# Dealing out a depthwise convolution's steps anew, unrolling four attention heads, and regrouping late conditioning loads

## The chip, the core and the metric

The kernel runs on one core of a Trainium2 chip. A core has TensorE (PE, matrix products into PSUM; PEld is its weight load), VectorE (DVE), ScalarE (ACT), GpSimd (POOL) and SyncE (SP), each with its own instruction queue, and 16 DMA engines that they share. The engines wait for each other through semaphores. The metric is the device time of one execution in microseconds, here the median of 3 runs; lower is better.

## The reference, cut to what matters

One decoder layer on 512 prompt tokens and 8 single-token samples, D_MODEL = 1024, all in float32:

```python
mod = c_act @ w_ada + b_ada                       # 9 x 1024 columns, conditioning of 3 norms and 3 gates
x = x + 0.5 * gt1 * swiglu(modulate(rms_norm(x), sh1, sc1), ...)
h = modulate(rms_norm(x), sh2, sc2)
ca, cb, q, k, v, r, a_lr, g_conv, g_gla = split(h @ w_in)
u = ca * sigmoid(cb)
d = causal_depthwise_conv(u, buf, conv_w) + conv_b           # 31 taps per channel
y_conv = silu(layer_norm(d)) @ w_conv_out
o, s_new = gla_chunked(q * HK ** -0.5, k, v, log_a, s0)      # 4 heads of linear attention
y_gla = (rms_norm(o) * silu(r)) @ w_gla_out
x = x + gt2 * ((sigmoid(g_conv) * y_conv + sigmoid(g_gla) * y_gla) @ w_out)
x = x + 0.5 * gt3 * swiglu(modulate(rms_norm(x), sh3, sc3), ...)
y = modulate(rms_norm(x), shf, scf)               # shf, scf = c_act @ w_ada_final + b_ada_final
```

## The kernel before, in words

Activations lie transposed in SBUF as 8 tiles (KT) of 128 channels by 520 columns (512 prompt tokens and 8 samples). The weights of every projection are worked through in *units*: one unit is 128 output channels, made of 48 matmuls of 260 columns (`unit`, L567 to L581; the matmuls show as L580). Each float32 operand is split into a high and a low part, and three products are formed. So a unit needs two weight tiles: `w_hi`, a cast on ACT (L1045), and `w_lo`, a subtraction on DVE (L1418) that waits for `w_hi`. Both are made in `step(n)`, which waits until unit n is done and then makes the weights of unit n+2 in the buffers that unit n has freed. PE therefore always has one unit in hand while the next but one is prepared. SP loads the raw weights, 1 MB for two units, and waits for `w_lo`.

The units of the mixing part come in this order: conv (16 units, which give u), qk (8), v (8), gates (24), then a layer norm over the convolution's output, yconv (8), ygla (8), out (8). What else happens is written by hand between the units of each engine:

- **The convolution.** It is done on DVE over four pairs of channel tiles. `conv_first(pair)` starts a pair with tap 0 (two instructions, L1706), and `conv_taps(pair, tap, count)` adds `count` taps, two instructions of 512 columns each (L1714, one per tile of the pair). Taps 1 to 30 of a pair follow each other. Pair 0 is done over the conv units, pair 1 over qk and v, pair 2 over v and gates, pair 3 over gates. Tables of counts, `TAPS_AT` (pair 3) and `TAPS2_AT` (pair 2), say how many taps follow each of the twelve gates units of a loop turn.
- **The decays** (`abs_z`, `log1p`, `decay`) run in the qk step: DVE makes |z|, ACT two passes of exp and ln for two heads at a time, DVE a scan over time.
- **The heads.** Six gates units (steps s = 0 to 5) go with each head. On every engine a hardware loop of two turns holds two heads each. Within a head DVE makes scaled copies of q and k (`diff`, `mix`), PE multiplies them (`gram`, L881), and DVE merges eight such results into the scores (`merge`, L1833). After unit s = 5 PE does the last two grams, then `prompt_o` (L941, L943), which waits for the eighth merge.
- **Conditioning.** The 44 slabs of 256 columns of `w_ada` and `w_ada_final` are multiplied with the conditioning vector. The first 32 go beside FFN 1. The last 12 (`LATE`) come in three stages of four slabs, at the norm before the mixing part, at the layer norm of the convolution, and at the norm before FFN 2. Of each stage `late_slabs` does the products on PE (L617), a copy brings the rows to SBUF, and `late_transposes` (L639) turns them into columns that DVE adds to `mod`. POOL loads the slabs into buffers that share memory with others: `raw_h`, the second half of stage 1, lies where `h_lo` is, which the gates units read until their end. So POOL waits for `s_done >= at["yconv"]` before that load.

After the last head the norm runs so: DVE adds up the eight tiles of d, PE sums over channels (L657), DVE subtracts the mean from each tile (L1941), ACT squares (L1346), PE sums the squares (L657), and ACT and DVE make the scale. On PE `late_slabs(1)` stands between the two sums.

Of the kernel before, what the change touches and what calls it, by code (L numbers as in the profile page):

```python
# [18 lines left out]
F32 = mybir.dt.float32  # L19
# [7 lines left out]
P = 128  # L27
# [26 lines left out]
TAPS_AT = [1, 2, 1, 1, 2, 0, 1, 2, 1, 2, 2, 0]  # L54
TAPS2_AT = [0, 0, 1, 1, 1, 2, 0, 0, 1, 1, 1, 0]
# [66 lines left out]
LATE_BANK = [0, 2, 0]  # L122
# [17 lines left out]
def decoder_step(nc, a, o):  # L140
# [3 lines left out]
    with ExitStack() as ctx:  # L144
# [22 lines left out]
        raw_h, h_lo = overlay(("raw_h", [P, 2, KT, 256], F32), ("h_lo", [P, KT, N], F32R))  # L167
# [40 lines left out]
        rows, o_hi, u = overlay(("rows", [P, 2 * D + 4 * P], F32), ("o_hi", [P, KT, N], F32R),  # L208
# [4 lines left out]
        rows_a, rows_l = lb[:, 0:2, 0:256], lb[:, 2:4, 0:NP]  # L213
# [41 lines left out]
        LATE = [((raw_a, "a1"), (raw_q, "q")), ((raw_v, "v2"), (raw_h, "h")), ((raw_a, "a3"), (raw_v, "v3"))]  # L255
# [30 lines left out]
        s_late = {k: sem("late_slabs_loaded_" + k) for k in ("a1", "q", "v2", "h", "a3", "v3")}  # L286
# [136 lines left out]
        def _(pool):  # L423
# [63 lines left out]
            def late_load(stage, two):  # L487

                dst, name = LATE[stage][two]
                for j in range(2):  # L490
                    m = LATE0 + 4 * stage + 2 * two + j
# [4 lines left out]
            late_load(0, 1)  # L496
            pool.wait_ge(s_ad, LATE0)
            late_load(0, 0)
# [25 lines left out]
            for h in range(HEADS):  # L524
                pool.wait_ge(s_S, 4 * h + 4)
                pool.dma_start(o["gla_p"][0, 0, h], SB[:, 3, :]).then_inc(s_So, 16)
                if h + 1 == HEADS:
                    pool.wait_ge(s_gk, HEADS)
                    late_load(1, 0)
# [22 lines left out]
            late_load(2, 0)  # L552
            late_load(2, 1)
# [5 lines left out]
        def _(pe):  # L559
# [61 lines left out]
            def late_slabs(stage):  # L621

                for two in range(2):
                    src, name = LATE[stage][two]
                    pe.wait_ge(s_late[name], 32)
                    for j in range(2):
                        last = slab_rows(src[:, j], 2 + two, 256 * j)
                    last.then_inc(s_lb, 1)

            def late_transposes(stage):  # L630

                pe.wait_ge(s_mod, LATE0 + 4 * stage)
                pe.wait_ge(s_lr, 2 * stage + 2)
                if stage == 1:
                    pe.wait_ge(s_or, 1)
                else:
                    pe.wait_ge(s_rstd, stage + 2)
# [105 lines left out]
            def ffn(which):  # L743
# [12 lines left out]
                for g in range(3):  # L756
                    n0 = at[f"up{which}_{g}"]
                    for i, k in bodies(pe, GROUPS[g] // 2, g == 0):
                        if g == 0 and i is None:
                            unit_pair(Lin(n0), h_hi, h_lo, s_h, (which - 1) * 3 * KT, rest if which == 1 else None)  # L760
                            if which == 2:
                                late_transposes(2)
# [1309 lines left out]
```

## Time and profile before

| | |
|---|---|
| median of 3 runs | 1534.94 us (1529.86, 1534.94, 1537.53) |
| the profiled execution | 1534.01 us |
| its span | 1531.3 us, 30166 instructions |
| mean granted TensorE clock | 0.976 |
| busy: PE / DVE / ACT / POOL | 94% / 53% / 32% / 5% |

The span is what the trace covers; the 2.7 us between it and the execution's own time lie outside. Busy time is what an engine's instructions took. The clock is a share of full speed, 1.0 for 2.4 GHz and 0.5 for 1.2 GHz. L numbers are lines of the kernel before.

### The profile page before, as it was taken

The page shows a single profiled execution, that of the slowest core. Times are in us where ns is not written, and L with a number is a line of the kernel's source. Part 1 is how long each engine was busy: PE and PEld are TensorE (multiplying, and loading weights), DVE is VectorE, ACT ScalarE, POOL GpSimd, SP SyncE. Part 2 cuts the span into 40 slices and gives each one's busy share as a digit, 9 for nine tenths or more (in the row PEclk, how much of TensorE's full clock was granted, in tenths as well). Part 3 has the DMA queues.
Part 4 walks back from the last instruction along what each step waited for, and adds up shares of the span by engine and source line. Part 5 has one row for each costly group of instructions (what it writes and reads, how often), then busy time and mean ns, then how long its engine had stood idle before and what let it go on. Part 6 is the DMA issues. An engine that isn't in the chain of part 4 may idle for free.

```text
span 1531.3 us, 30166 instructions
## 1 busy us (share of the span) xinstructions
PE 1445.2 (94%) x11974; PEld 1395.4 (91%) x11974; DVE 817.1 (53%) x1362; ACT 483.0 (32%) x651; POOL 75.8 (5%) x112
## 2 busy tenths in 40 slices
PE   6999999999998999999988995999989999999995
PEld 5899999999997999988988894999989999999994
DVE  5423332333365785999696795765552332333345
ACT  5322122212245225233323234522342212221233
POOL 6100000010000000000000001000000000000000
PEclk9999999999999999999999998999999999999997
DMA  9754545474232222222332445334313223223211
GB/s 308 228 185 137 192 138 185 138 260 127 68 100 87 83 92 78 83 83 94 132 116 80 138 149 168 136 115 154 125 52 107 85 83 103 89 83 99 87 62 56
DMA packets 133332, 187.10 MB, mean 122 GB/s; under 512 B 4571, under 2 KB 113519, under 8 KB 133214
## 3 DMA queue, kind: packets, MB, share of 16 engines
q1 hardware_dynamic: 112396, 112.54, 23.1%
q0 software_dynamic: 16800, 64.85, 12.7%
q10 hardware_dynamic: 4050, 8.53, 1.5%
q8 instruction: 59, 0.97, 0.3%
q14 instruction: 27, 0.22, 0.0%
HBM read 172.44 MB, written 14.41 MB: 122 GB/s over the span
## 4 chain that ended last, share of the span: by engine, by line
PE 53%; DVE 9%; issue 4%; ACT 2%; DMA 1%; DVEq 1%; POOL 0%; ACTq 0%
PE pu L580 45%; PE pu L596 3%; DVE d L1714 1%; DVE w_lo L1418 1%; DMA raw_h<-in_w_ada_final 1%; ACT w_hi L1045 1%; PE pg L657 1%; DVE work L1833 1%; DVE work L1842 1%; PE pg L941 1%; PE pg L881 1%; DVE work L1826 0%; PE pg L995 0%; DVE sg L1547 0%; DVE work L1814 0%
## 5 line engine op out<-in xcount | busy, mean ns | idle before, releaser
L1418 DVE TENSOR_TENSOR w_lo<-raw,w_hi 128x1024 fp32r<-128x1024 f32 x216 | 264.2, 1224 | 575.5 <-ACT w_hi L1045 575.4
L580 PE MATMUL pu<-h_hi,w_hi 128*128 128x260 f32 x2432 | 497.7, 286 | 12.3 <-issue 6.5
L580 PE MATMUL pu<-h_hi,w_lo 128*128 128x260 f32 x2432 | 492.4, 284 | 0.0
L580 PE MATMUL pu<-h_lo,w_hi 128*128 128x260 f32 x2432 | 491.3, 284 | 0.0
L1045 ACT CAST w_hi<-raw 128x1024 fp32r<-128x1024 f32 x216 | 225.8, 1046 | 664.3 <-PE pu L580 648.1
L580 PEld LDWEIGHTS pu<-h_hi,w_hi 128*128 128x128 f32 x2432 | 377.6, 190 | 17.7 <-issue 10.5
L580 PEld LDWEIGHTS pu<-h_hi,w_lo 128*128 128x128 f32 x2432 | 377.3, 190 | 0.0
L580 PEld LDWEIGHTS pu<-h_lo,w_hi 128*128 128x128 f32 x2432 | 376.7, 189 | 0.0
L1714 DVE SCALAR_TENSOR_TENSOR d<-u,cw,d 128x512 f32<-128x512 f32 x240 | 162.7, 743 | 0.0
L580 PE MATMUL pu<-f_hi,w_hi 128*128 128x260 f32 x704 | 142.6, 284 | 2.0 <-DVE f_lo L1669 2.0
L580 PE MATMUL pu<-f_hi,w_lo 128*128 128x260 f32 x704 | 141.8, 283 | 0.0
L580 PE MATMUL pu<-f_lo,w_hi 128*128 128x260 f32 x704 | 141.3, 282 | 0.0
L580 PEld LDWEIGHTS pu<-f_hi,w_hi 128*128 128x128 f32 x704 | 108.3, 188 | 4.1 <-DVE f_lo L1669 2.5
L580 PEld LDWEIGHTS pu<-f_hi,w_lo 128*128 128x128 f32 x704 | 108.4, 188 | 0.0
L580 PEld LDWEIGHTS pu<-f_lo,w_hi 128*128 128x128 f32 x704 | 108.3, 188 | 0.0
L1176 ACT CAST f_hi<-sg 128x520 f32 (+1 forms) x44 | 27.6, 627 | 87.8 <-DVE sg L1666 87.8
L1669 DVE TENSOR_TENSOR f_lo<-sg,f_hi 128x520 f32 (+1 forms) x44 | 30.8, 701 | 40.4 <-ACT f_hi L1176 40.4
L596 PE MATMUL pu<-h_hi,w_hi 128*128 128x260 f32 x128 | 29.0, 312 | 11.7 <-DVE h_lo L1565 6.6
L1286 ACT ACTIVATE work<-work 128x512 f32<-128x512 f32 x28 | 17.7, 631 | 68.2 <-DVE work L1814 68.1
L881 PEld LDWEIGHTS pg<-work 128*128 128x128 f32 x224 | 27.1, 191 | 8.5 <-DVE work L1833 4.8
L596 PEld LDWEIGHTS pu<-h_hi,w_hi 128*128 128x128 f32 x128 | 22.2, 212 | 13.3 <-issue 13.0
L881 PE MATMUL pg<-work 128*128 128x128 f32 x224 | 30.6, 282 | 3.2 <-DVE work L1833 3.2
(283 smaller groups left out, 1287.7 us busy)
## 6 DMA issues: line engine op xcount, KB each, us to landing
raw_a<-in_w_ada POOLq DMA_DIRECT2D x30, 1024.0 KB, 7.8
raw<-in_w_in SPq DMA_DIRECT2D x28, 1024.0 KB, 5.2
raw<-in_ffn_up SPq DMA_DIRECT2D x22, 1024.0 KB, 5.4
raw<-in_ffn_gate SPq DMA_DIRECT2D x21, 1024.0 KB, 5.4
raw<-in_ffn_down SPq DMA_DIRECT2D x16, 1024.0 KB, 4.9
gates_d<-sg ACTq DMA_DIRECT2D x24, 260.0 KB, 2.1
raw<-in_ffn_down SPq DMA_DIRECT2D x8, 768.0 KB, 4.2
work<-gates_d POOLq DMA_DIRECT2D x2, 2080.0 KB, 11.4
```

Of the source, the lines that this page charges most:

```text
L580: last = mm(pu[p][:, e, 0:HALF], w[p][:, k, :], m[:, k, e * HALF:(e + 1) * HALF], start=(k == 0 and j == 0), stop=(k == k_tiles - 1 and j ...
L596: last = mm(pu[p][:, e, 0:HALF], w[p][:, k, :], m[:, k, e * HALF:(e + 1) * HALF], start=(k == 0 and j == 0), stop=(k == KT - 1 and j == 2))
L657: last = mm(ps[:, e, 0:HALF], ones[:], src[:, e * HALF:(e + 1) * HALF], start=start, stop=stop)
L881: last = mm(pg[:, l % 2, c * CH:(c + 1) * CH], m, m if rhs is None else rhs[:, c * CH:(c + 1) * CH], start=True, stop=True)
L941: last = mm(pg[:, 2 + t, cs], VH[:, c, ts], SC[:, cs], start=True, stop=(c == 0))
L1045: nc.scalar.copy(w_hi[p][:], raw[:, slot, :, p * P:(p + 1) * P]).then_inc(s_hi, 1)
L1176: nc.scalar.copy(tile(f_hi, Lin(2 * k0 + c - 2, 2, i).value()), sg[:, c - 2, :]).then_inc(s_ahi, 1)
L1286: af(E_[:, l % 2, :], E_[:, l % 2, :], ACT.Exp, scale=1 / 16).then_inc(s_ge, 1)
L1418: V.tensor_tensor(w_lo[p][:], raw[:, slot, :, p * P:(p + 1) * P], w_hi[p][:].bitcast(F32), ALU.subtract).then_inc(s_lo, 1)
L1669: V.tensor_tensor(tile(f_lo, t.value()), s, tile(f_hi, t.value()).bitcast(F32), ALU.subtract).then_inc(s_a, 1)
L1714: conv.mark(V.scalar_tensor_tensor(d[:, t, 0:NP], flat(u[:, t:t + 1, bass.ds(tap + s, NP)]), cw[:, bass.ds((tap + s) * KT + t, 1)], d[:, t ...
L1833: V.copy_predicated(SC.rearrange("p (c t) -> p c t", c=NC), masks[:, l:l + 1, :].bitcast(U16).to_broadcast([P, NC, CH]), pg[:, l % 2, :].r ...
```

## The change

Four things are done together.

1. **Taps.** The 120 taps stay, in the same order for each pair, but stand elsewhere on DVE: 18 instead of 14 in the qk step, 28 instead of 30 in the v step, 44 instead of 46 over the heads. Pair 1 starts with three taps ahead of the first qk unit and three more stand in qk's step 2. Over the heads one table now gives, for each of the six steps, 1, 1, 2, 2, 0, 7 taps in heads 0 to 2 and 1, 1, 2, 1, 0, 0 in head 3 (before: 1, 2, 2, 2, 3, 2 in heads 0 and 2, and 1, 2, 2, 3, 3, 0 in heads 1 and 3).
2. **Heads.** PE and DVE have their four heads written out instead of a loop of two turns with two heads each. ACT keeps its loop. The five additions of d at the end of a turn are now issued once, not twice.
3. **ACT's order.** In the qk step the second `log1p` comes after the next unit's cast and copy, not before. In the v step the copy out of PSUM of each fourth unit comes before the cast of the next weights.
4. **Late slabs.** Six slabs go over the first of the three norms, two over the layer norm, four over the last. `raw_h` is gone. The new buffer `raw_u` lies where `u` will be; POOL issues its load right after that of `raw_q`.

```diff
-TAPS_AT = [1, 2, 1, 1, 2, 0, 1, 2, 1, 2, 2, 0]
-TAPS2_AT = [0, 0, 1, 1, 1, 2, 0, 0, 1, 1, 1, 0]
+TAPS_AT = [1, 1, 2, 2, 0, 7] * 3 + [1, 1, 2, 1, 0, 0]
+TAPS_V = [(2, 2), (1, 2), (2, 2), (1, 2)]
-        LATE = [((raw_a, "a1"), (raw_q, "q")), ((raw_v, "v2"), (raw_h, "h")), ((raw_a, "a3"), (raw_v, "v3"))]
+        LATE = [(raw_a, "a1"), (raw_q, "q"), (raw_u, "u"), (raw_v, "v2"), (raw_a, "a3"), (raw_v, "v3")]
 # POOL
-            late_load(0, 1)
+            late_load(1)
+            pool.wait_ge(s_tp, 4 + KT)
+            late_load(2)
             pool.wait_ge(s_ad, LATE0)
-            late_load(0, 0)
+            late_load(0)
...
-                if h + 1 == HEADS:
-                    pool.wait_ge(s_done, at["yconv"])
-                    late_load(1, 1)
 # PE, first conv units
                     unit_pair(Lin(at["conv"]), h_hi, h_lo, s_h, KT)
-                    late_transposes(0)
-                    pe.wait_ge(s_mod, LATE0 + 4)
+                    pe.wait_ge(s_lr, 1)
+                    late_slabs(2)
+                    pe.wait_ge(s_rstd, 2)
+                    late_transposes(0, 1)
...
             a_rows()
+            late_transposes(2)
 # PE, heads
-            with pe.Fori(0, 2) as i:
-                for hh in range(2):
-                    h = Lin(hh, 2, i)
+            for hh in range(HEADS):
+                h = Lin(hh)
...
             pe.wait_ge(s_oe, 2 * HEADS)
-            late_slabs(1)
+            late_slabs(3)
 # ACT, qk and v steps
-                        if c >= 2:
-                            log1p((2 * c - 4, 2 * c - 3))
+                        if c == 2:
+                            log1p((0, 1))
+                    elif c == 0:
+                        log1p((2, 3))
...
-                    step(Lin(at["v"] + c, 4, i))
+                    n = Lin(at["v"] + c, 4, i)
+                    act.wait_ge(s_done, n.value(1, 1))
+                    if c < 3:
+                        step(n)
                     nc.scalar.copy(halves(sg[:, c, :]), psum(c % 2)).then_inc(s_evac[c % 2], 1)
+                    if c == 3:
+                        step(n)
 # DVE, qk step
             conv_first(1)
+            conv_taps(1, 1, 3)
...
                 if c == 1:
-                    conv_taps(1, 1, 2)
+                    conv_taps(1, 4, 2)
                 if c == 2:
                     abs_z(0)
                     abs_z(1)
+                    conv_taps(1, 6, 3)
...
-                conv_taps(1, 3 + 3 * c, 3)
-                if c == 0:
-                    decay(2)
-                    decay(3)
+                if c in (1, 2):
+                    decay(c + 1)
+                conv_taps(1, (9, 12, 13, 15)[c], (3, 1, 2, 4)[c])
 # DVE, heads
+            def gate_taps(done, count):
+
+                for k in range(done, done + count):
+                    if k < 14:
+                        conv_taps(2, 17 + k, 1)
+                    else:
+                        conv_taps(3, k - 13, 1)
...
-                        conv_taps(2, i * 8 + (15 + sum(TAPS2_AT[:c])), TAPS2_AT[c])
-                        conv_taps(3, i * 15 + (1 + done), more - done)
+                    gate_taps(sum(TAPS_AT[:6 * hh + s]), TAPS_AT[6 * hh + s])
 # DVE, layer norm
-            for two in range(2):
-                dve.wait_ge(s_lb, two + 3)
-                V.tensor_copy(rows_l[:, two], pg[:, 2 + two, :]).then_inc(s_lr, 1)
+            dve.wait_ge(s_lb, 4)
+            V.tensor_copy(rows_l[:, LATE_SLOT[3]], pg[:, LATE_ROWS[3], :]).then_inc(s_lr, 1)
```

How the instructions stand, at three places. DVE before, in head 0, from the last tap of step 4 over step 5 (`w_lo`, two merges) to its first tap:

```order
L102 REGISTER_ALU
L1714 ISA
L1714 SCALAR_TENSOR_TENSOR d<-u,cw,d 128x512
L1417 REGISTER_ALU
L1418 TENSOR_TENSOR w_lo<-raw,w_hi 128x1024
L1914 REGISTER_ALU
L1833 COPY_PREDICATED work<-masks,pg 128x512
L1831 REGISTER_ALU
L1833 COPY_PREDICATED work<-masks,pg 128x512
L102 REGISTER_ALU
L1714 ISA x2
L1714 SCALAR_TENSOR_TENSOR d<-u,cw,d 128x512
```

DVE now, in head 1, from the last merges of step 4 to the first unit of head 2 (taps are L1727, merges L1852, `w_lo` L1433):

```order
L1935 TENSOR_SCALAR work<-qk 128x512
L1852 COPY_PREDICATED work<-masks,pg 128x512
L1433 TENSOR_TENSOR w_lo<-raw,w_hi 128x1024
L1852 COPY_PREDICATED work<-masks,pg 128x512 x2
L1727 SCALAR_TENSOR_TENSOR d<-u,cw,d 128x512 x14
L1433 TENSOR_TENSOR w_lo<-raw,w_hi 128x1024
L1888 TENSOR_TENSOR work<-lb 128x512
```

The taps between merge 5 and `w_lo` have gone; fourteen tap instructions stand behind the eighth merge. The register instructions that worked out addresses from the loop's counter have gone too.

PE before, from the end of the loop over the heads to the layer norm's sums:

```order
L943 MATMUL pg<-work 128x128
L946 REGISTER_ALU
L946 COMPARE_AND_BRANCH
L657 MATMUL pg<-sg,ones 128x260 x2
L617 MATMUL pg<-raw_v,c_f 32x256 x16
L617 MATMUL pg<-raw_h,c_f 32x256 x16
L657 MATMUL pg<-sg,ones 128x260 x16
L995 MATMUL pg<-work,ones 128x260 x4
```

PE now:

```order
L946 MATMUL pg<-work 128x128
L948 MATMUL pg<-work 128x128
L655 MATMUL pg<-sg,ones 128x260 x2
L618 MATMUL pg<-raw_v,c_f 32x256 x16
L655 MATMUL pg<-sg,ones 128x260 x16
L999 MATMUL pg<-work,ones 128x260 x4
```

The products with `raw_h` have gone from here, and so has the branch. The products with `raw_u` now stand behind the first pair of conv units.

ACT before, in the qk step, from the copy of unit 3 (L1242) to that of unit 4 (`w_hi` is L1045, `log1p` L1232 and L1236):

```order
L1242 ACTIVATE qk<-pu 128x520
L1232 ACT_TABLE_LOAD
L1232 ACTIVATE sg<-sg 128x520 x2
L1236 ACT_TABLE_LOAD
L1236 ACTIVATE sg<-sg,ones 128x520 x2
L114 UNCONDITIONAL_BRANCH
L1045 CAST w_hi<-raw 128x1024
L1242 ACTIVATE qk<-pu 128x520
```

ACT now:

```order
L1250 ACTIVATE qk<-pu 128x520
L114 UNCONDITIONAL_BRANCH
L1051 CAST w_hi<-raw 128x1024
L1250 ACTIVATE qk<-pu 128x520
L1240 ACT_TABLE_LOAD
L1240 ACTIVATE sg<-sg 128x520 x2
```

The cast `w_hi` for the second next unit stands ahead of the exp and ln passes now.

## Rows read from the trace of the kernel before

**Rows 1.** Page, part 1: busy us (share of the span) xinstructions.

```profile
PE 1445.2 (94%) x11974; PEld 1395.4 (91%) x11974; DVE 817.1 (53%) x1362; ACT 483.0 (32%) x651; POOL 75.8 (5%) x112
```

**Rows 2.** Windows: length, busy (x instructions) per engine, PEclk, DMA share, GB/s.

```profile
612.00:620.00 8.00, 6.19 (x39) 6.19 (x39) 7.43 (x13) 2.34 (x4) 0.00 (x0) 0.79 0.00 0
683.12:803.21 120.09, 112.56 (x867) 106.88 (x865) 101.71 (x184) 37.61 (x58) 4.74 (x6) 0.96 0.36 116
736.06:744.33 8.27, 5.86 (x29) 5.87 (x29) 4.75 (x7) 0.17 (x1) 0.92 (x1) 0.59 0.72 244
794.83:815.60 20.77, 13.34 (x79) 13.15 (x79) 6.46 (x9) 1.18 (x2) 1.78 (x2) 0.75 0.51 155
862.78:868.54 5.76, 3.38 (x31) 3.39 (x31) 4.72 (x7) 0.17 (x1) 0.90 (x1) 1.00 0.62 176
918.87:955.52 36.65, 21.02 (x137) 15.61 (x137) 19.63 (x30) 14.54 (x21) 4.07 (x5) 0.86 0.55 175
```

**Rows 3.** Timeline, PE, qk step: start, us, instruction, [idle before].

```profile
613.81 0.51 PE L580 MATMUL pu<-h_hi,w_hi 128*128 128x260 f32 x2 [2.05 <-DVE w_lo L1418]
622.92 0.51 PE L580 MATMUL pu<-h_hi,w_hi 128*128 128x260 f32 x2 [1.57 <-DVE w_lo L1418]
```

**Rows 4.** Timeline, DVE and ACT, the same step.

```profile
607.46 0.67 DVE L1762 SCALAR_TENSOR_TENSOR sg<-lb 128x520 f32<-128x520 f32 x1
612.53 1.23 DVE L1418 TENSOR_TENSOR w_lo<-raw,w_hi 128x1024 fp32r<-128x1024 f32 x1 [4.40 <-ACT w_hi L1045]
...
611.37 1.03 ACT L1045 CAST w_hi<-raw 128x1024 fp32r<-128x1024 f32 x1
```

**Rows 5.** Timeline, PE and ACT, v step.

```profile
654.76 0.63 PE L862 MATMUL pg<-ident,sg 128*128 128x128 f32 x4 [1.67 <-issue]
...
681.16 0.59 ACT L1261 COPY sg<-pu 128x520 f32<-128x520 f32 x1
```

**Rows 6.** Timeline, PE, heads 0 and 3.

```profile
712.38 1.16 PE L881 MATMUL pg<-work 128*128 128x128 f32 x8 [1.60 <-DVE work L1833]
...
922.17 1.22 PE L941 MATMUL pg<-work 128*128 128x128 f32 x4 [3.30 <-DVE work L1833]
```

**Rows 7.** Timeline, DVE, head 0, steps 4 and 5.

```profile
731.64 4.05 DVE L1714 SCALAR_TENSOR_TENSOR d<-u,cw,d 128x512 f32<-128x512 f32 x6
735.61 1.23 DVE L1418 TENSOR_TENSOR w_lo<-raw,w_hi 128x1024 fp32r<-128x1024 f32 x1
737.62 0.72 DVE L1833 COPY_PREDICATED work<-masks,pg 128x512 f32<-128x512 uint16 x1 [0.15 <-DVE work L1833]
751.44 1.22 DVE L1418 TENSOR_TENSOR w_lo<-raw,w_hi 128x1024 fp32r<-128x1024 f32 x1 [10.48 <-ACT w_hi L1045]
```

**Rows 8.** Chain that ended last: a whole unit, and the loop's jump back.

```profile
744.55 5.78 PE pu L580 x48
803.21 4.08 issue
807.28 8.31 PE pu L580 x48
```

**Rows 9.** The same chain, between the heads and the convolution's output matmul.

```profile
921.34 15.81 DMA raw_h<-in_w_ada_final
937.20 3.64 PE pg L617 x32
940.84 7.86 PE pg L657 x32
955.52 13.24 PE pu L596 x96
```

**Rows 10.** Timeline, DVE and ACT, the same place.

```profile
929.28 4.97 DVE L1941 TENSOR_TENSOR d<-d,sg 128x520 f32<-128x520 f32 x8
...
943.48 0.64 ACT L1346 ACTIVATE sg<-d 128x520 f32<-128x520 f32 x1 [0.24 <-PE pg L657]
```

**Rows 11.** DMA queue q8 (instructions), 683.1 to 803.2: packets, MB, share.

```profile
q8 instruction: 7, 0.11, 0.4%
```

More of the change, by code:

```diff
@@ L619, in slab_rows, with late_slabs, late_transposes @@
                 return last
-            def late_slabs(stage):
-                for two in range(2):
[L624 to L637, printed above, removed]
-                for j in range(8):
-                    last = mm(pg[:, LATE_BANK[stage], 10 * j:10 * j + 10], rows_l[:, j // 4, j % 4 * P:(j % 4 + 1) * P],
-                              sel[:], start=True, stop=True)
+            def late_slabs(g):
+                src, name = LATE[g]
+                pe.wait_ge(s_late[name], 32)
+                for j in range(2):
+                    last = slab_rows(src[:, j], LATE_ROWS[g], 256 * j)
+                last.then_inc(s_lb, 1)
+            def late_transposes(*groups):
+                pe.wait_ge(s_mod, LATE0 + 2 * groups[0])
+                pe.wait_ge(s_lr, groups[-1] + 1)
+                for g in groups:
+                    for j in range(4):
+                        c = 10 * (j + 4 * (g - groups[0]))
+                        last = mm(pg[:, LATE_BANK[g], c:c + 10], rows_l[:, LATE_SLOT[g], j * P:(j + 1) * P],
+                                  sel[:], start=True, stop=True)
                 last.then_inc(s_lt, 1)
@@ L778, in _ @@
             late_slabs(0)
+            late_slabs(1)
             def state_transposes(t0):
                 pe.wait_ge(s_ld["st"], 32)
-                pe.wait_ge(s_rstd, 2)
+                pe.wait_ge(s_mod, LATE0 + 4)
+                pe.wait_ge(s_lr, 3)
                 for t in range(t0, t0 + 4):
@@ L819, in _ @@
             a_rows()
+            late_transposes(2)
             def u_tails():
+                pe.wait_ge(s_mod, LATE0 + 6)
                 for p in range(2):
@@ L1721, in conv_units @@
                     step(n)
+                    if i is None and c == 1:
+                        late_out(0, 1)
+                        dve.wait_ge(s_lb, 3)
+                        chain.link(V.memset(u[:, :, 0:TAPS - 1], 0.0))
                     if c >= 2:
@@ L1739, in _ @@
             conv.end(3)
+            late_out(2)
             def sample_conv():
@@ L1789, in _ @@
                 step(Lin(at["qk"] + 4 + c))
-                conv_taps(1, 3 + 3 * c, 3)
-                if c == 0:
-                    decay(2)
-                    decay(3)
+                if c in (1, 2):
+                    decay(c + 1)
+                conv_taps(1, (9, 12, 13, 15)[c], (3, 1, 2, 4)[c])
             conv_first(2)
             with dve.Fori(0, 2) as i:
-                conv.loop(i, 30)
+                conv.loop(i, 28)
                 for c in range(4):
                     step(Lin(at["v"] + c, 4, i))
-                    conv_taps(1, i * 8 + (15 + 2 * c), 2)
-                    conv_taps(2, i * 7 + (1 + 2 * c), 2 if c < 3 else 1)
+                    for pair, at_0, per, j in ((1, 19, 6, 0), (2, 1, 8, 1)):
+                        conv_taps(pair, i * per + (at_0 + sum(t[j] for t in TAPS_V[:c])), TAPS_V[c][j])
             conv.end(2)
```

267 lines of the change are left out of this document (133 added, 134 removed).

## The prediction

> **What bounds the kernel now.** I read the page's busy times first. PE is busy 94% of the span and everything else far less [rows 1], so the kernel is as long as PE's work plus its pauses and its slow stretches. Next the chain that ended last: it runs through PE's units almost everywhere and leaves PE only in the mixing part, so I cut that part into stretches and asked of each how long PE stood and at which clock [rows 2]. A whole unit takes 5.78 us at full clock [rows 8]. Then the timelines say who ended each pause. The reader is to see five kinds of pause in these rows: two in the qk step that end with `w_lo` [rows 3, 4], one after each fourth v unit [rows 5], one in the middle of a head and one ahead of `prompt_o` that both end with a merge on DVE [rows 6], one where the loop over the heads jumps back [rows 8], and a long one at the layer norm that ends with the load of `raw_h` [rows 9]. After several of them the granted clock is at its lower level, 1.2 GHz: 0.79 on the mean over 612 to 620, 0.59 after the pause of head 0 [rows 2].
>
> **The qk step.** DVE has its last |z| ready at 607.46 + 0.67, then stands 4.40 us because ACT does both passes of `log1p` before it casts `w_hi` at 611.37 [rows 4]. Unit 5 ended at 613.81 - 2.05 = 611.8 and unit 4 one unit earlier [rows 3, 8], at 606, so with the cast first it is ready by 607.2 and `w_lo` follows at 608.1, well ahead of 611.8, when PE wants it. The 2.05 us go. The second pause, 1.57 us, came because three taps and two decays stood between two `w_lo`; now the decays stand one unit apart. Each of the next slots holds at most one `w_lo` (1.2) and three taps (six instructions, 4.05), or one `w_lo`, a decay (its instructions took about 2) and two taps (2.7), against 5.8 us of PE. The clock over the 8 us was 0.79: 0.21 of 8 us, 1.7 us, come back with the first pause. The six taps added earlier lie in idle time of DVE before units 0 and 3. Sum 2.05 + 1.57 + 1.7 = 5.3 us; bounds 3.6 (the clock stays as it was) and 5.4.
>
> **The v step.** PE stands 1.67 us for the copy that follows the cast [rows 5]. The copy takes 0.59 us, the cast 1.03 [rows 4, 5]. With the copy first the pause is 0.65; twice 1.0 is 2.0 us. The cast comes 0.6 us later, where the unit that wants it is 7 us away. The two taps fewer change nothing, since DVE is not waited for. Bounds 1.5 and 3.0.
>
> **Middle of heads 0 and 2.** PE waits 1.60 us for merge 0 in each [rows 6]. DVE works without a gap up to it, and one tap of two instructions less stands ahead of it: 4.05 / 6 = 0.675 us an instruction [rows 7], 1.35 us. 2 x 1.35 = 2.7 us; bounds 0 and 3.2.
>
> **Ends of heads 0, 1 and 2.** The three stretches run from the last small matmul before `prompt_o` [rows 2]. The first and third are 8.27 and 5.76 us and end with `prompt_o`; the second is 20.77 us and takes in the jump and the next unit. At full clock `prompt_o` keeps PE busy 3.38 us (third stretch, clock 1.00). The pause ahead of it is there because six tap instructions, 4.05 us, end at 735.6 and only then come `w_lo` and two merges [rows 7]. Without them `w_lo` is done before the last gram is, which ends about when the stretch begins less 1.1 us; two merges take 0.15 + 2 x 0.72 = 1.6, and leave a pause of 0.7 with their hand-over. So the first and third stretch become 0.7 + 3.4 = 4.1, and the second, whose 4.08 us of jump have gone and whose unit took 8.31 instead of 5.78 us [rows 8], becomes 4.1 + 5.8 = 9.9. Gain 4.2 + 1.7 + 10.9 = 16.8 us. The lower bound is 10 us: the three pauses shrink, the jump goes, and the clock falls as before. What is late next are the 14 tap instructions behind the eighth merge: 14 x 0.675 = 9.45 us, from 0.7 to 10.2 us after the stretch's begin. The `w_lo` behind them can start only when the next unit has ended and its `w_hi` is cast: 4.1 + 5.8 + 1.05 = 10.9. They fit with 0.7 us to spare, in a place where DVE stood for 10.48 us [rows 7]. The tap's mean over the page's list would be 0.743 us by the single instruction; pipelined in runs it is 0.675, and this is a run.
>
> **The layer norm.** From the end of the small matmuls of head 3 to the first matmul of yconv it is 36.65 us [rows 2]. Two things go. The pause of 3.30 us ahead of `prompt_o` [rows 6] shrinks to 0.7, and the additions of d follow the same merges, so all moves up by 2.6. And the load of `raw_h`, which lands at 937.15 [rows 9], is gone with its products. The squares' sums ended at 940.84 + 7.86 = 948.70. What is late next is the chain of the squares: the first centred tile is there at 929.28 + 4.97 / 8 = 929.9, its square 0.64 later, and then one sum each 0.64 + 0.24 = 0.88 us [rows 10]: 930.6 + 8 x 0.88 = 937.6. The remaining products with `raw_v` are over by 930.4, as now. So 948.7 - 937.6 = 11.1, with the 2.6 together 13.7 us. `raw_v` is issued when head 3's states are made, 24 us ahead of this place, and the reload of the gates (2 MB, 11.4 us in the page's list) is wanted after the pair of yconv units. Bounds: 8 us, if PE does the eight sums and the slabs at the lower clock after its short pauses, and 15.
>
> **The slabs themselves.** The layer norm's transposes shrink from 8 to 4, 0.8 us less. At the first norm two slabs and four transposes are added, 1.9 + 0.8 us, on PE. In turn PE no longer waits there for DVE to write `mod` (`s_mod` LATE0 + 4), which with the hand-over costs about the same. I take 0 for it, between a gain of 2 and a loss of 3. The load into `raw_u` is issued some hundred microseconds ahead of its use.
>
> **The sum.** 5.3 + 2.0 + 2.7 + 16.8 + 13.7 + 0.8 = 41.3 us. The profiled execution took 1534.01 us, 0.9 below the median shown; less 41.3 that is 1492.7. Forecast 1492.7 us. All low bounds together give 3.6 + 1.5 + 0 + 10 + 8 + 0.8 - 3 = 20.9, 1513; all high ones 5.4 + 3 + 3.2 + 18 + 15 + 0.8 + 2 = 47, 1487.
>
> **Rivals.** *First: DVE takes the place of the pauses in the heads.* In two heads it is busy 101.71 of 120.09 us now, and 184 instructions stand there [rows 2]. If the heads shorten to about 110 us and 26 taps instead of 23 stand in them, DVE is busy some 102 of 110 us. For it speaks that little is left for hand-overs, and that the seven taps fit with only 0.7 us. Against it: in steps 0 to 4, where PE waits for DVE's merges, DVE has 6 taps instead of 10. If the burst comes 2.5 us late at three ends, and the clock falls each time for another 1.7 us, 12.6 us are lost again: 1505.
>
> *Second: the layer norm keeps its length.* Another transfer or the low clock takes over from `raw_h`. For it: PE still has pauses of about 2 and 5 us there, and its clock over the whole stretch is 0.86 [rows 2]. Against it, nothing else waited for lands after 937. With 8 instead of 13.7, and the same caution at the heads' ends (10 instead of 16.8), the time is 1505 as well.
>
> *Third, on the other side: straight code stalls as the jump did.* PE's jump back costs 4.08 us of issue with nothing waited for, and the next unit 2.5 us of clock [rows 8], 6.6 together. The unrolled heads 2 and 3 are code that no one has fetched. During heads 0 and 1, q8 brought 7 packets of instructions [rows 11]. If each such packet stalled PE as the jump did, 7 x 6.6 = 46 us would be lost and 41.3 won: 1539. It decides from six such stalls on. Against it: heads 0 and 1 are run for the first time in that very stretch, with the 7 packets, and no pause of theirs over half a microsecond is "issue"; the price seems that of a jump to a place that isn't at hand, not of going on.
>
> The Trainium skill, "Advanced Engine Details and Errata", section ISA Cache, gives TensorE 128 KB in lines of 16 KB, 256 instructions each. By that figure the 867 matmuls and 865 weight loads of two heads are about 7 lines, as many as the q8 packets, which agrees with the trace. The same section says "Only 2 cache lines!". By that rule the code of heads 0 and 1 is never at hand when the loop returns, which fits the stall at the jump, and unrolled code would stall only if fetching ahead fails; the trace shows that it does not in heads 0 and 1.
>
> *Fourth: the change gives nothing*, because the pauses were ended by something else that stands as before. Nothing in the rows supports it; 1530.
>
> **Chances.** Forecast 0.74, first rival 0.10, second 0.08, third 0.05, fourth 0.03. A range of 1484 to 1511 holds the first three cases and leaves out less than 2 in 10. I count about 0.5% (7.7 us) as what can't be told from no change. Faster 0.92, the same 0.04, slower 0.04.
>
> **What would show it.** Right: no wait of PE for DMA at the layer norm, and the stretch from `prompt_o`'s small matmuls to yconv near 23 us; no "issue" pause between heads 1 and 2; the pauses ahead of `prompt_o` near 0.7 us; two v pauses of 0.65; no pause for `w_lo` in qk; DVE without the 10 us hole after each head; mean clock above 0.98. Wrong: PE waiting for `w_lo` in the first units of a head (first rival), a low clock through the sums of squares (second), "issue" pauses spread over the heads (third), or a new wait at the first conv units, where I put 0.

## The result and the profile after

The changed kernel takes 1493.18 us, the median of four runs (1491.07 to 1494.09). The kernel before, run beside it, takes 1532.71 us. The ratio is 0.9739, with a 95% interval of 0.9717 to 0.9762: 2.6% faster. The forecast was 1492.7 us. The profiled execution took 1494.09 us, of which its span is 1492.5 us; the span of before was 1531.3 us.

The page's busy row of the changed kernel, which answers to [rows 1], and its chain by engine:

```profile
PE 1434.5 (96%) x11974; PEld 1387.0 (93%) x11974; DVE 814.3 (55%) x1357; ACT 483.8 (32%) x652; POOL 74.5 (5%) x112
...
PE 60%; DVE 6%; ACT 2%; issue 1%; ACTq 0%; DVEq 0%
```

PE has the same 11974 matmuls and is busy 10.7 us less: the mean granted clock rose from 0.976 to 0.982, so it does less of the same work at the lower clock. The span is 38.8 us shorter; the other 28.1 us of it are idle time that has gone.

Next the windows, in the same columns as [rows 2]. The first fence is of the kernel before: its qk step, and its four heads from the first gate unit to the last small matmul of head 3. The second is of the changed kernel: its qk step, the same 8 us in it as in [rows 2], its four heads, and its layer norm.

```profile
572.69:628.70 56.01, 52.39 (x408) 51.43 (x409) 40.36 (x72) 24.60 (x32) 1.01 (x2) 0.97 0.25 79
683.12:918.87 235.75, 220.06 (x1705) 208.92 (x1703) 191.73 (x351) 73.51 (x113) 9.41 (x12) 0.96 0.37 120
```

```profile
571.60:622.10 50.50, 50.50 (x410) 49.95 (x411) 45.46 (x81) 24.02 (x31) 1.01 (x2) 1.00 0.27 85
612.00:620.00 8.00, 8.00 (x69) 8.00 (x68) 6.98 (x13) 2.52 (x4) 0.00 (x0) 1.00 0.43 133
674.38:895.28 220.90, 217.52 (x1705) 207.00 (x1703) 189.26 (x344) 73.89 (x113) 9.43 (x12) 0.98 0.38 128
895.28:918.72 23.44, 15.44 (x105) 12.37 (x105) 16.73 (x27) 14.83 (x21) 2.32 (x3) 0.94 0.50 182
```

In the qk step PE now stands for nothing, and the clock is whole: in the 8 us from 612 on it is busy 8.00 us at a clock of 1.00, where it was busy 6.19 us at 0.79. In the heads the length less PE's busy time is the idle time: 235.75 - 220.06 = 15.69 us before, 220.90 - 217.52 = 3.38 us after. The same subtraction is used below for every experiment. The layer norm took 36.65 us [rows 2] and takes 23.44.

The timeline of PE in the changed kernel, at the places of [rows 5, 6]: the v step, the middle and the end of head 0, the end of head 1 with the first units of head 2, the end of head 3, and the layer norm.

```profile
647.00 0.63 PE L867 MATMUL pg<-ident,sg 128*128 128x128 f32 x4 [0.73 <-issue]
...
702.01 1.13 PE L886 MATMUL pg<-work 128*128 128x128 f32 x8
...
723.67 1.06 PE L886 MATMUL pg<-qk,work 128*128 128x128 f32 x8
724.59 1.05 PE L935 MATMUL pg<-sel_o,work 128*128 128x4 f32 x8
726.65 0.71 PE L946 MATMUL pg<-work 128*128 128x128 f32 x4 [1.00 <-DVE work L1852]
...
781.35 0.71 PE L946 MATMUL pg<-work 128*128 128x128 f32 x4 [1.01 <-DVE work L1852]
781.89 0.39 PE L948 MATMUL pg<-work 128*128 128x128 f32 x2
...
783.18 1.06 PE L946 MATMUL pg<-work 128*128 128x128 f32 x4
784.04 0.64 PE L948 MATMUL pg<-work 128*128 128x128 f32 x2
...
786.03 0.58 PE L581 MATMUL pu<-h_hi,w_hi 128*128 128x260 f32 x2
...
896.28 0.71 PE L946 MATMUL pg<-work 128*128 128x128 f32 x4 [1.00 <-DVE work L1852]
...
901.27 1.14 PE L655 MATMUL pg<-sg,ones 128*128 128x260 f32 x4 [1.60 <-DVE sg L1957]
902.34 1.93 PE L618 MATMUL pg<-raw_v,c_f 128*32 128x256 f32 x32
904.61 7.28 PE L655 MATMUL pg<-sg,ones 128*128 128x260 f32 x32 [0.33 <-ACT sg L1361]
```

No bracket stands at the unit of 786.03 us, where before the loop jumped back: the 4.08 us of issue [rows 8] are gone. The pauses ahead of `prompt_o` (L946) are 1.00 us instead of 2.41, 3.36, 2.38 and 3.30 us. But look at the rows from 781.89 on: two small matmuls take 0.39 us, and a moment later 0.64. That is the clock falling to 1.2 GHz after a pause of 1.01 us. After head 0, with the same pause, it did not fall. At the layer norm only one product with a slab stands between the sums, and none waits for a load; [rows 9] had 15.81 us of it.

DVE at the ends of heads 0 and 1, which answers to [rows 7]:

```profile
722.96 1.23 DVE L1433 TENSOR_TENSOR w_lo<-raw,w_hi 128x1024 fp32r<-128x1024 f32 x1 [1.67 <-ACT w_hi L1051]
724.99 1.60 DVE L1852 COPY_PREDICATED work<-masks,pg 128x512 f32<-128x512 uint16 x2 [0.81 <-PE pg L886]
726.49 9.35 DVE L1727 SCALAR_TENSOR_TENSOR d<-u,cw,d 128x512 f32<-128x512 f32 x14
737.03 1.23 DVE L1433 TENSOR_TENSOR w_lo<-raw,w_hi 128x1024 fp32r<-128x1024 f32 x1 [1.19 <-ACT w_hi L1051]
...
793.44 1.23 DVE L1433 TENSOR_TENSOR w_lo<-raw,w_hi 128x1024 fp32r<-128x1024 f32 x1 [2.90 <-ACT w_hi L1051]
```

The 14 tap instructions take 9.35 us and fill the hole of 10.48 us. `w_lo` behind them waits for ACT's cast and not for the taps. It is also seen why the pause ahead of `prompt_o` is 1.00 us: both merges wait until the last gram has ended, 0.81 us after DVE became free, and only then run, one behind the other, in 1.60 us.

### The profile page after: what moved, and what is told of

It is laid out like the page before. It is cut to its first block, busy times and chain, and to the rows that moved or that the text cites. A ratio compares the mean times of both kernels' runs of the same rounds, so it can differ in the third digit from the quotient of the medians.

```text
span 1492.5 us, 29632 instructions
## 1 busy us (share of the span) xinstructions
PE 1434.5 (96%) x11974; PEld 1387.0 (93%) x11974; DVE 814.3 (55%) x1357; ACT 483.8 (32%) x652; POOL 74.5 (5%) x112
## 4 chain that ended last, share of the span: by engine, by line
PE 60%; DVE 6%; ACT 2%; issue 1%; ACTq 0%; DVEq 0%
PE pu L581 50%; PE pu L597 3%; PE pg L886 2%; PE pg L916 1%; DVE w_lo L1433 1%; PE pg L655 1%; ACT w_hi L1051 1%; PE pg L946 1%; DVE work L1852 0%; DVE sg L1562 0%; PE pg L948 0%; PE pg L902 0%; DVE qk L1997 0%; DVE o_lo L2005 0%; DVE qk L1999 0%
## 5 line engine op out<-in xcount | busy, mean ns | idle before, releaser
L1433 DVE TENSOR_TENSOR w_lo<-raw,w_hi 128x1024 fp32r<-128x1024 f32 x216 | 264.4, 1225 | 553.8 <-ACT w_hi L1051 553.4
L1727 DVE SCALAR_TENSOR_TENSOR d<-u,cw,d 128x512 f32<-128x512 f32 x240 | 162.6, 743 | 0.0
L1090 ACT ACTIVATE sg<-x 128x520 f32<-128x520 f32 x24 | 15.3, 639 | 56.4 <-DVE x L1594 56.4
L431 POOL DMA_DIRECT2D raw_a<-in_w_ada x24 | 21.1, 884 | 249.0 <-PE pg L618 248.2
```

The costliest lines, as they stand in the source:

```text
L431: pool.dma_start(dst, v[:, :, bass.ds(c, 256)]).then_inc(s_loaded, 16)
L1090: af(sg[:, t.base % 2, :], tile(src, t.value()), ACT.Square).then_inc(s_sq, 1)
L1433: V.tensor_tensor(w_lo[p][:], raw[:, slot, :, p * P:(p + 1) * P], w_hi[p][:].bitcast(F32), ALU.subtract).then_inc(s_lo, 1)
L1727: conv.mark(V.scalar_tensor_tensor(d[:, t, 0:NP], flat(u[:, t:t + 1, bass.ds(tap + s, NP)]), cw[:, bass.ds((tap + s) * KT + t, 1)], d[:, t ...
```

## The experiments

All ratios are to the kernel before, run beside each; its median was 1532.71 us beside after, 1533.45 beside the first four experiments and 1533.84 beside the last four. To keep the parts apart, this table gives every kernel's median and, for the stretch of the four heads, the length, PE's busy time and the idle time, from one window of each profile.

| kernel | median us | ratio (95%) | heads, us | PE busy | idle |
|---|---|---|---|---|---|
| before | 1532.71 | | 235.75 | 220.06 | 15.69 |
| slabs alone | 1523.26 | 0.9935 (0.9917 to 0.9954) | 236.00 | 220.74 | 15.26 |
| heads written out alone | 1528.15 | 0.9972 (0.9960 to 0.9985) | 229.36 | 220.22 | 9.14 |
| after | 1493.18 | 0.9739 (0.9717 to 0.9762) | 220.90 | 217.52 | 3.38 |
| after, slabs as before | 1504.42 | 0.9831 (0.9804 to 0.9858) | 217.94 | 214.56 | 3.38 |
| after, PE's heads a loop | 1500.36 | 0.9793 (0.9772 to 0.9814) | 223.84 | 218.13 | 5.71 |
| after, taps of the heads nearly as before | 1497.93 | 0.9777 (0.9752 to 0.9802) | 224.97 | 214.58 | 10.39 |
| after, ACT's order as before | 1496.36 | 0.9746 (0.9728 to 0.9764) | 217.97 | 214.59 | 3.38 |
| after, merges split | 1485.75 | 0.9683 (0.9669 to 0.9697) | 214.42 | 212.73 | 1.69 |
| the same, additions early | 1485.46 | 0.9687 (0.9671 to 0.9703) | 214.49 | 212.79 | 1.70 |

The intervals are 4 to 8 us wide from end to end. Those of the old taps and of ACT's old order overlap the interval of after, so their 4.75 and 3.2 us are not told apart from nothing by the times alone. What carries them is the pauses that come back in their profiles.

**The slabs alone.** The kernel before with the six, two and four slabs regrouped; taps, loops and ACT's order as before. The core of the edit:

```diff
-        LATE = [((raw_a, "a1"), (raw_q, "q")), ((raw_v, "v2"), (raw_h, "h")), ((raw_a, "a3"), (raw_v, "v3"))]
+        LATE = [(raw_a, "a1"), (raw_q, "q"), (raw_u, "u"), (raw_v, "v2"), (raw_a, "a3"), (raw_v, "v3")]
```

> The kernel before with only the late slabs regrouped six, two, four. Theory (the wait for raw_h is a pause of its own, whatever the heads do): PE's wait for DMA at the layer norm goes, the squares' sums end about 11 us sooner, transposes give 0.8, the start of the conv units about 0.9: 12.5 us less, 1520, and no other stretch changes. Rival (the layer norm has a second cause close behind): no more than 6 us less, 1527.

Measured: 10.2 us less than the kernel before beside it, where 12.5 had been expected, and 10.6 us of span. At the layer norm the wait for `raw_h` is gone and 0.91 us is left ahead of the sums of the squares:

```profile
926.60 1.93 PE L618 MATMUL pg<-raw_v,c_f 128*32 128x256 f32 x32
929.44 7.28 PE L655 MATMUL pg<-sg,ones 128*128 128x260 f32 x32 [0.91 <-ACT sg L1355]
```

From the end of the small matmuls of head 3 to yconv it is 25.05 us (918.49 to 943.54) instead of 36.65. Of these 11.6 us 1.5 are a shorter pause ahead of `prompt_o`, 1.84 instead of 3.30, which the slabs do not touch; 10.1 are left for the slabs. The two pauses of the qk step (2.06 and 3.08 us), those of the heads (idle 15.26 us) and the jump (3.63 us of issue) all remain. So this part acts by itself, at its own place.

One of these numbers deserves a look. The second pause of the qk step is 3.08 us here and 1.57 in the kernel before, and yet nothing is lost: from the end of the first pause to the end of the second it is 9.09 us here (611.96 to 621.05) and 9.11 before (613.81 to 622.92). DVE's `w_lo` sets that time. In the kernel before PE worked at the lower clock inside it and so had less left to wait; low clock ahead of a pause that another engine ended cost nothing here.

**The heads written out alone.** The kernel before, with the loops of PE and DVE over two passes of two heads replaced by straight code:

```diff
-            with pe.Fori(0, 2) as i:
+            for i in range(2):
                 for hh in range(2):
-                    h = Lin(hh, 2, i)
+                    h = Lin(2 * i + hh)
```

> The kernel before with only PE's and DVE's heads written out, taps and slabs as before. Theory (the 4.08 us of issue are the price of the loop's jump back): the pause between heads 1 and 2 loses 4.1 us and the next unit about 2.5 us of low clock, 6.6 us less in all, 1526; the pauses for the merges stay. Rival (code run for the first time stalls): issue pauses in heads 2 and 3, the same time or longer, 1532 to 1575.

Measured: 1528.15 us, 5.3 us less than before beside it; 6.6 had been expected. No pause of "issue" appears in heads 2 and 3, so the rival is out. In the heads the idle time falls by 6.55 us, of which 4.08 are the jump. PE's busy time does not fall at all (220.22 against 220.06). Three windows show why; they run from the pause in the middle of head 0 to `prompt_o`, from `prompt_o` of head 1 over the jump to the middle of head 2, and from `prompt_o` of head 2 to the end. First the kernel before, then this one:

```profile
712.38:738.47 26.09, 23.68 (x184) 21.38 (x185) 25.94 (x49) 7.07 (x11) 0.92 (x1) 0.98 0.25 79
798.19:839.08 40.89, 35.10 (x250) 34.10 (x250) 23.20 (x42) 10.90 (x17) 1.45 (x2) 0.87 0.36 113
865.16:918.87 53.71, 53.71 (x433) 51.35 (x433) 44.13 (x83) 17.93 (x27) 3.22 (x4) 1.00 0.50 170
```

```profile
714.65:740.69 26.04, 25.04 (x185) 22.90 (x185) 25.86 (x49) 7.20 (x11) 0.42 (x1) 0.93 0.25 78
798.85:832.79 33.94, 32.44 (x250) 31.74 (x250) 23.32 (x42) 10.92 (x17) 1.45 (x2) 0.95 0.45 142
858.71:915.10 56.39, 56.39 (x433) 54.04 (x433) 44.55 (x83) 17.93 (x27) 3.22 (x4) 0.95 0.48 162
```

At the jump 6.95 us are won, pause and clock together, close to the 6.6 expected. But after `prompt_o` of head 2 the clock falls, which it had not done before, and 2.7 us are lost again. In the first window PE's pause ahead of `prompt_o` is 1.00 instead of 2.41 us and the stretch is as long as it was: DVE sets its length, and PE, at the lower clock for a part of it, comes later to the same wait.

**The change without its slabs.** Taps, heads and ACT's order of after, slabs grouped as before.

```diff
-        LATE = [(raw_a, "a1"), (raw_q, "q"), (raw_u, "u"), (raw_v, "v2"), (raw_a, "a3"), (raw_v, "v3")]
+        LATE = [((raw_a, "a1"), (raw_q, "q")), ((raw_v, "v2"), (raw_h, "h")), ((raw_a, "a3"), (raw_v, "v3"))]
```

> The changed kernel with the late slabs grouped and loaded as before (raw_h back). Theory (additive): PE waits again for raw_h at the layer norm, some 13 to 14 us more in that stretch because the heads now end sooner against the same load, about 1506 in all. Rival (the gains of the heads made it cheaper): 5 us more or less, 1498.

Measured: 1504.42 us, 11.2 us above after, where 13 to 14 had been expected. The load is back, and PE waits 5.87 us for it:

```profile
908.20 3.64 PE L617 MATMUL pg<-raw_h,c_f 128*32 128x256 f32 x32 [5.87 <-DMA raw_h<-in_w_ada_final]
```

The stretch at the layer norm is 33.12 us here (893.32 to 926.44) against 23.44: with the other parts in place the slabs are worth 9.7 us there, alone 10.1. So they add up with the rest almost without loss. The 11.2 us of the medians hold other things too: the heads, whose code is that of after, are 2.96 us shorter here by the clock, and the rest of the difference lies ahead of them, behind the layer norm and in the spread of the runs.

**The change with PE's heads as a loop.** Only PE's part of the heads goes back to two passes; DVE's stays written out.

```diff
-            for hh in range(HEADS):
-                h = Lin(hh)
+            with pe.Fori(0, 2) as i:
+                for hh in range(2):
+                    h = Lin(hh, 2, i)
```

> The changed kernel with only PE's heads as a loop of two turns again, DVE's heads written out and taps as changed. Theory: one pause of issue of about 4.1 us between heads 1 and 2 and up to 2.5 us of low clock behind it: 1497 to 1500. Rival (it was DVE's loop, not PE's): 1493, no such pause.

Measured: 1500.36 us, 7.2 us above after. The pause at the jump is back, and as DVE's heads are written out here it is PE's own; it is 2.35 us and not the 4.1 expected:

```profile
790.65 0.50 PE L581 MATMUL pu<-h_hi,w_hi 128*128 128x260 f32 x2 [2.35 <-issue]
```

The idle time of the heads rises by 2.33 us, the pause itself, and the busy time by 0.6. The rest of the 7.2 us lies outside the heads: PE reaches the gates 1.8 us later than in after (of these 0.9 by 425 us of the trace), 1.0 us is lost behind the heads, and 1.4 us outside the span. I have no reason for these from the edit. To the loop belong, as far as the trace shows it, the 2.9 us in the heads.

**The taps of the heads nearly as before.** The change, with the table of the taps over the heads put back as far as it goes: heads 0 to 2 have their old counts, while head 3 has two taps fewer in step 4 than it had (1 instead of 3), because 44 taps are dealt there now and not 46. So the pauses of heads 0 to 2 are tested, that of head 3 is not.

```diff
-TAPS_AT = [1, 1, 2, 2, 0, 7] * 3 + [1, 1, 2, 1, 0, 0]
+TAPS_AT = [1, 2, 2, 2, 3, 2, 1, 2, 2, 3, 3, 0, 1, 2, 2, 2, 3, 2, 1, 2, 2, 3, 1, 0]
```

> The changed kernel with the 44 taps over the heads dealt nearly as before (1, 2, 2, 2, 3, 2 in heads 0 and 2, 1, 2, 2, 3, 3, 0 in head 1, 1, 2, 2, 3, 1, 0 in head 3). Theory (three taps ahead of w_lo and the last merges hold up prompt_o): pauses of 2.4 and 3.4 us ahead of prompt_o in heads 0 to 2 again, 1.6 us in the middle of heads 0 and 2, and more low clock: 8 to 14 us more, 1501 to 1507. Rival (unrolling alone cured the heads' ends): under 3 us more, 1493 to 1496.

Measured: 1497.93 us, 4.75 above after; 8 to 14 had been expected. The pauses do come back, as expected, 1.45 us in the middle of heads 0 and 2 and 2.25, 2.85 and 2.27 ahead of `prompt_o`: idle 10.39 us against 3.38, so 7.0 us more.

```profile
703.24 1.13 PE L886 MATMUL pg<-work 128*128 128x128 f32 x8 [1.45 <-DVE work L1852]
729.15 0.71 PE L946 MATMUL pg<-work 128*128 128x128 f32 x4 [2.25 <-DVE work L1852]
```

But PE is busy 2.9 us less (214.58 against 217.52). With longer pauses this kernel runs at the lower clock for a shorter time than after does. The clock that I had expected to be lost beside each pause was not; that part of the theory fails here. The rival fails as well: writing out the heads did not cure their ends, the taps did.

**ACT's order as before.** The change, with both passes of `log1p` ahead of the cast in the qk step and the cast ahead of the copy in the v step. Of the edit, the part in the qk step:

```diff
-                        if c == 2:
-                            log1p((0, 1))
-                    elif c == 0:
-                        log1p((2, 3))
+                        if c >= 2:
+                            log1p((2 * c - 4, 2 * c - 3))
```

> The changed kernel with ACT's order in the qk and v steps as before, all taps and decays where the change put them. Theory (ACT's late cast made the pauses): 2 us and its low clock in qk, 2 x 1.0 us in v: 4 to 7 us more, 1497 to 1500. Rival (the decays' new places alone cured qk): only v's 2 us, 1495.

Measured: 1496.36 us, 3.2 above after; 4 to 7 had been expected. One pause is back in the qk step, with its low clock (0.79 over 611 to 619 us), and two of 1.67 us in the v step:

```profile
613.12 0.51 PE L581 MATMUL pu<-h_hi,w_hi 128*128 128x260 f32 x2 [2.06 <-DVE w_lo L1426]
```

The second pause of qk, 1.57 us before, is not: that one went with the new places of taps and decays, not with ACT's order. PE reaches the gates 6.25 us later than in after (680.63 against 674.38). In the heads, whose code is the same and whose idle time is the same 3.38 us, it wins back 2.9 us by the clock alone.

**The two last merges split.** If the pause of 1.00 us is the wait for the last gram and two merges, and if it is what the clock falls after, it should help to let the merge of gram 6 go ahead while gram 7 runs:

```diff
-                        dve.wait_ge(s_gg, h.value(8, 8))
+                        dve.wait_ge(s_gg, h.value(8, 7))
                         dve.sem_inc(s_merge, 1)
                         merge(h, 6)
+                        dve.wait_ge(s_gg, h.value(8, 8))
                         merge(h, 7)
```

> The changed kernel, but merge 6 waits for gram 7 alone (the seventh of eight) and only merge 7 for the last gram. Theory (the 1.0 us left ahead of prompt_o is two merges behind the last gram, and it is also what the clock falls after): the pause shrinks from 1.0 to 0.2 us in all four heads, 3.2 us, and one or more of the low stretches behind it go, 1.7 us each: 1485 to 1490. Rival (the merges are not what PE waits for, or the clock falls anyway): 1490 to 1493.

Measured: 1485.75 us (1484.90 to 1486.11), ratio 0.9683 (0.9669 to 0.9697). The interval lies wholly below that of after, so this version beats both kernels, and the time is in the 1485 to 1490 expected. Its windows, at the end of head 1, over the heads and at the layer norm, and PE's row at the end of head 3:

```profile
779.20:783.40 4.20, 3.79 (x33) 3.82 (x34) 4.20 (x8) 0.49 (x2) 0.90 (x1) 1.00 1.02 339
...
673.86:888.28 214.42, 212.73 (x1704) 202.15 (x1703) 189.61 (x346) 73.81 (x113) 9.44 (x12) 1.00 0.40 131
...
888.28:911.00 22.72, 15.58 (x106) 12.52 (x106) 16.15 (x26) 14.98 (x21) 2.32 (x3) 0.98 0.53 189
```

```profile
888.74 0.68 PE L946 MATMUL pg<-work 128*128 128x128 f32 x4 [0.43 <-ACT qk L1335]
```

The pause is 0.43 us (0.2 had been expected) and no longer ends with a merge but with ACT's copy. The clock is 1.00 over all four heads. The heads become 6.5 us shorter than in after: 1.7 us of idle time, 4.8 us of clock. A pause that was shortened by 0.57 us four times gave 7.4 us. How much of the clock is due to it is less sure: the same heads as in after, with the same pauses of 1.00 us, had PE busy 214.6 us in two other kernels and 217.5 in after, so the split merges are worth between 1.8 and 4.8 us of clock.

**The additions of d early.** The kernel just shown, with the five additions of d for the layer norm moved from step 5 of head 3 into its steps 3 and 4, to take away the 1.30 us that PE waits there for them:

```diff
-                    if hh == HEADS - 1 and s == 5:
-                        for t in range(5):
+                    if hh == HEADS - 1 and s in (3, 4):
+                        for t in range(2) if s == 3 else range(2, 5):
```

> As the last one, and the five additions of d stand in steps 3 and 4 of head 3 instead of behind the last merge. Theory: the channel sum follows prompt_o at once, 1.6 us less at the layer norm, 1483 to 1488. Rival (they delay w_lo and the merges of step 5 in head 3): as the last one or slower.

Measured: 1485.46 us, not told apart from the 1485.75 before it, where 1.6 us less had been expected. PE's mean sum has no pause now, but the sums of the squares begin at 896.30 instead of 896.74 us, with 0.98 us of pause where 0.33 was. PE's rows, and ACT's ahead of the first square:

```profile
892.05 1.04 PE L655 MATMUL pg<-sg,ones 128*128 128x260 f32 x4
893.39 1.93 PE L618 MATMUL pg<-raw_v,c_f 128*32 128x256 f32 x32 [0.30 <-ACT qk L1338]
896.30 7.28 PE L655 MATMUL pg<-sg,ones 128*128 128x260 f32 x32 [0.98 <-ACT sg L1361]
```

```profile
892.32 1.01 ACT L1338 COPY qk<-pg 128x1024 f32 x1 [3.62 <-PE pg L948]
893.36 1.28 ACT L1344 ACT_TABLE_LOAD   x1
894.65 1.07 ACT L1347 ACTIVATE work<-qk 128x1040 f32<-128x1040 f32 x1
895.63 1.67 ACT L1361 ACTIVATE sg<-d 128x520 f32<-128x520 f32 x3
```

The first centred tile is there 1.46 us earlier, but ACT is busy with the copy of `qk`, a table load and one activation until the square. The wait was handed from DVE to ACT; 0.44 us is left of 1.30.

## Why the prediction was right

The time, the direction and the places are right: 1492.7 us forecast, 1493.18 measured. The forecast was counted down from the profiled execution by 41.3 us; the two profiled executions differ by 39.9. That the total is only half a microsecond off owes something to luck, as the terms show. Term by term, from one trace to the other:

**The qk step**, 5.3 us forecast: its 56.0 us (572.69 to 628.7) became 50.5 (571.60 to 622.1), 5.5 less. Both pauses and the low clock went: 3.6 us of idle time and 1.9 of busy time. The run with ACT's old order, where only the first pause came back, shows that ACT's order was the cause of the first. The second stayed away there, so it went with the new places of the taps and decays; no run took these back by themselves in the qk step.

**The v step**, 2.0 forecast: 2.15. The pause is 0.73 us, forecast 0.65.

**The heads**, 2.7 in the middle and 16.8 at the ends, 19.5 forecast: 14.85 measured, and this is the one term that was mis-sized. It splits cleanly. In pauses the forecast was 2.7 for the middle, 2.41 + 3.36 + 2.38 - 3 x 0.7 = 6.05 ahead of `prompt_o`, and 4.08 for the jump, 12.8 us; idle time fell by 12.3. The pauses ahead of `prompt_o` are 1.00 where 0.7 was forecast, because the last gram ends at 723.67 + 1.06 = 724.73, only 0.9 us ahead of the end of the small matmuls (I had 1.1), and the merges begin 0.26 us after it. The rest of the forecast, 19.5 - 12.8 = 6.7 us, was clock; 2.5 came. The step that failed is "at full clock", in the ends of the heads: I took the stretches as 0.7 + 3.4 with the clock whole, since the shortest pause ahead of `prompt_o` (2.38 us) had left it at 1.00 and longer ones had not. It fell none the less in three places: at 783 and at 841 us, after pauses of 1.01 and 0.99, and at 817 us in the middle of head 2, with no pause over 0.3 us near it. Windows of the second and third, with the stretch ahead of the one at 817:

```profile
813.50:816.90 3.40, 3.26 (x20) 2.53 (x18) 3.40 (x9) 1.05 (x2) 0.00 (x0) 1.00 0.11 39
816.90:820.30 3.40, 3.40 (x16) 3.32 (x16) 3.40 (x6) 1.64 (x3) 0.00 (x0) 0.51 0.00 0
840.80:844.20 3.40, 3.40 (x19) 3.40 (x18) 3.40 (x6) 0.00 (x0) 0.00 (x0) 0.51 1.07 407
```

These are windows of the changed kernel; the third number from the end, 1.00 and twice 0.51, is the clock. The split merges show the size: with 0.43 us of pause the heads run at 1.00 and give back 4.8 us, somewhat more than the 4.2 that were missing. But the fall is not bound to the pause of 1.00 us alone. With the same heads and pauses, the change without its slabs and the one with ACT's old order had a single low stretch, after `prompt_o` of head 0, and 5.5 of the 6.7 us came.

**The layer norm**, 13.7 forecast: 13.2, 36.65 to 23.44. The slabs, 11.1 forecast, are worth 10.1 us there alone and 9.7 with the rest; of the remaining 3 us 2.3 are the shorter pause ahead of `prompt_o` (3.30 to 1.00). As the working said, the chain of the squares is late next, and then it runs without a gap: 7.28 us for the eight sums, where 8 x 0.88 = 7.04 had been taken. Between it and yconv PE has a pause of 5.07 us that was there before and is untouched.

**The transposes and the first norm**, 0.8 and 0 forecast: about 3 in all. From the pair of yconv units to the end it is 2.0 us shorter, 573.78 against 575.78. Most of that is chance: with the slabs alone, whose code there is that of after, the same stretch is 577.16 us long, and PE is busy 552.8 us in it against 549.5, so the clock moves it by more than the change does. At the convolution PE reaches the qk step 0.9 us earlier, although it does two slabs and four transposes more (L618 1.93 us, and L637): with the old slabs it waited 2.44 us between the pair and the next unit, which I had set equal to the added work of 2.7 us without a row for it.

```profile
485.06 0.77 PE L580 MATMUL pu<-h_hi,w_hi 128*128 128x260 f32 x2 [2.44 <-issue]
```

```profile
480.69 1.93 PE L618 MATMUL pg<-raw_u,c_f 128*32 128x256 f32 x32
...
484.36 0.48 PE L581 MATMUL pu<-h_hi,w_hi 128*128 128x260 f32 x2
```

The first of these rows is of before, the others of after. So the misses cancelled: the heads were 4.65 us short and the layer norm 0.5, while these small terms gave 2.3 us more than forecast (3.1 with 0.2 us of an earlier start, against 0.8), qk and v 0.35, and 1.1 us went outside the span, for which there was no term. Two slips in the working did no harm: the lowest sum gave 1513 us, and yet the range ended at 1511; and the highest sum took 18 us for the heads' ends, a bound that stands nowhere before it.

**The rivals.** DVE does not take the place of the pauses: `w_lo` behind the 14 tap instructions waits for ACT, and DVE is busy 93.04 of 105.96 us in heads 0 and 1. The layer norm does not keep its length. Straight code does not stall: in heads 2 and 3 PE shows no pause of issue, while the instruction queue brings 7 packets, as it does in heads 0 and 1. Here that row, for 780.34 to 895.28 us of after:

```profile
q8 instruction: 7, 0.11, 0.5%
```

With the loop kept, the second pass brought 8 packets (803 to 923 us of before): its code was fetched again. The Trainium skill, "Advanced Engine Details and Errata", section ISA Cache, has it that only two lines of 256 instructions are held, and by that rule a body of 1732 matmuls and weight loads must be fetched anew in each pass; the 8 packets agree. What the rule leaves out is the price: about the same number of packets costs nothing in straight code and a pause of 2.35 to 4.08 us at a jump. That the fetching is what PE waits for at the jump is likely by this but not shown. What the forecast took from the first run of heads 0 and 1 was enough to decide the rival.

## What stays open

Which pauses the lower clock follows is not settled. The heads of after, of the change without its slabs and of the change with ACT's old order are the same code with the same 3.38 us of idle time, and PE is busy 217.52, 214.56 and 214.59 us in them. The mean clock of a whole execution is nearly the same in all runs of one kernel (0.982, 0.983, 0.983 and 0.983 for after), so the difference is hardly noise of one run; but the heads by themselves were seen in one profile of each kernel. What differs there is when the heads begin (674.38, 675.38 and 680.63 us). With the old taps, pauses of 1.45 to 2.85 us cost less clock than after's pauses of 1.00. The single removals therefore are not the parts of a sum: 11.2 + 7.2 + 4.75 + 3.2 = 26.4 us of 39.5. Most of that gap is this clock: in three of the four removals PE is busy 2.9 to 3.0 us less in the heads than in after, 8.8 us together, and in two of them the heads' code is untouched. The rest, 4.3 us, is within what the medians leave open; besides, no run took back the dealing of taps in qk and v or the pause of head 3, so the parts were not all removed. Nor was it looked into why PE is later at 425 us with the loop.

## What to carry to other kernels

Where one engine sets the time and the throttle follows its pauses, split each stretch into its idle time and its busy time at the granted clock, and forecast the two apart; here the first came out within half a microsecond over four heads (12.8 forecast, 12.3 measured), the second did not (6.7 and 2.5), and needs a bound from both sides. Ask also which engine sets the length of a stretch: in the qk step low clock ahead of a pause that DVE ends only shortened the pause. A pause that remains small is still worth removing when it is repeated: look whether the merge, copy or cast that ends it waits for more than it needs. Work that fills an engine's holes belongs behind the result that another engine waits for, not ahead of it. Before buying back a pause, look one step further down: when DVE's additions left, ACT's table load was there. And judge a removal by what happens at its own place: the total also holds the clock of places that it doesn't touch.

## What the runs showed of the hardware that I had not expected

The clock fell to its lower level after pauses as short as 1.0 us, and once among small matmuls with no pause over 0.3 us, and was 1.00 over 214 us of heads with pauses of 0.43 us. In the qk step low clock ahead of a wait for DVE cost nothing (9.11 us with it, 9.09 without). A jump back over PE's body of two heads costs 4.08, 3.63 and 2.35 us of issue in three kernels with the same body, so its price is no constant; straight code of the same length costs none.
